# A mixture-of-experts loop over 32-token groups: from pairs to quads of groups, with one gather and one scatter for four, in the experts' natural order

## What is computed

```python
    def expert_block(args):
        rows, wts, e = args
        hgu = tok[rows] @ w_gu[e] + b_gu[e]
        gate = jnp.minimum(hgu[:, 0::2], SWIGLU_LIMIT)
        up = jnp.clip(hgu[:, 1::2], -SWIGLU_LIMIT, SWIGLU_LIMIT)
        act = (up + 1.0) * (gate * jax.nn.sigmoid(SWIGLU_ALPHA * gate))
        y = act @ w_down[e] + b_down[e]
        return y.astype(jnp.float32) * wts[:, None]
```

## Time and profile before

| | |
|---|---|
| median of 3 runs | 1428.87 us |
| the profiled execution | 1430.1 us, span 1428.3 us |
| mean granted TensorE clock | 0.917 |
| PE busy | 1201.5 us, 84% of the span |
| DVE, ACT busy | 266.6 us (19%), 230.9 us (16%) |
| chain that ended last | PE 60%, DMA 34%, issue 3% |
| DMA | 455.98 MB, mean 319 GB/s |

### The profile page before, as it was taken

How to read it: one execution, slowest core, us unless ns; L and a number is a source line. 1 busy time by engine, 2 the same in 40 slices (tenths; PEclk the granted TensorE clock), 3 DMA queues, 4 the chain that set the end, 5 groups by cost and what they waited for, 6 DMA issues and landing times.

```text
span 1428.3 us, 19043 instructions
## 1 busy us (share of the span) xinstructions
PE 1201.5 (84%) x7477; PEld 540.9 (38%) x7478; DVE 266.6 (19%) x786; ACT 230.9 (16%) x529; POOL 18.5 (1%) x26
## 2 busy tenths in 40 slices
PE   8999999999799766899999778696788797976677
PEld 4655868885433212333333122132222232312122
DVE  3335243632411100111111001010111011100001
ACT  2134423350111000111111011011011111100001
POOL 1100010000000000000000000000000000000000
PEclk9999999999799898989998989899898899988989
DMA  9933264223898999948527989989999999899993
GB/s 344 314 118 118 77 250 145 78 98 139 347 377 358 426 424 425 420 170 344 244 118 323 424 337 427 428 356 426 427 413 426 428 417 428 346 425 425 427 424 129
DMA packets 66265, 455.98 MB, mean 319 GB/s; under 512 B 7284, under 2 KB 13016, under 8 KB 33432
## 3 DMA queue, kind: packets, MB, share of 16 engines
q1 hardware_dynamic: 65528, 454.13, 77.6%
q0 software_dynamic: 256, 0.79, 0.2%
q10 hardware_dynamic: 448, 0.60, 0.1%
HBM read 454.45 MB, written 1.05 MB: 319 GB/s over the span
## 4 chain that ended last, share of the span: by engine, by line
PE 60%; DMA 34%; issue 3%; DVE 1%; ACT 1%; SPq 0%; ACTq 0%; DVEq 0%
DMA ring<-in_w_down 29%; PE bank L1005 16%; PE bank L1032 9%; PE bank L557 6%; PE bank L697 6%; DMA ring<-in_w_gu 5%; PE bank L972 4%; PE bank L980 4%; PE bank L991 2%; PE bank L606 2%; PE bank L893 2%; PE bank L859 2%; PE bank L546 1%; PE bank L583 1%; PE bank L881 1%
## 5 line engine op out<-in xcount | busy, mean ns | idle before, releaser
L1005 PE MATMUL bank<-ring,sp_ 128*32 128x512 f32 x2944 | 409.7, 688 | 134.0 <-DMA ring<-in_w_gu 80.2
L1032 PE MATMUL bank<-ring,mq 128*32 128x512 f32 x1472 | 184.5, 635 | 65.0 <-DMA ring<-in_w_down 62.6
L1005 PEld LDWEIGHTS bank<-ring,sp_ 128*32 128x32 f32 x2944 | 91.4, 119 | 372.3 <-issue 245.7
L1775 DVE TENSOR_SCALAR sp_<-bank 128x256 f32<-128x256 f32 x46 | 19.5, 425 | 858.5 <-PE bank L1005 858.5
L1032 PEld LDWEIGHTS bank<-ring,mq 128*32 128x32 f32 x1472 | 46.3, 114 | 195.5 <-issue 100.4
L972 PEld LDWEIGHTS bank<-sp_,sc 128*128 128x128 f32 x736 | 88.0, 199 | 24.3 <-issue 24.3
L972 PE MATMUL bank<-sp_,sc 128*128 128x64 f32 x736 | 91.1, 284 | 2.0 <-DVE sp_ L1758 2.0
L980 PE MATMUL bank<-mq,sp_ 128*128 128x512 f32 x184 | 86.1, 611 | 1.5 <-ACT sp_ L1363 1.5
L557 PE MATMUL bank<-ring 128*128 128x512 f32 x192 | 83.2, 592 | 0.0
L1336 ACT ACTIVATE mq<-bank 64x512 f32<-64x512 f32 x46 | 27.1, 589 | 318.6 <-PE bank L1032 318.6
L697 PE MATMUL bank<-ring 128*128 128x256 f32 x320 | 71.3, 381 | 0.0
(11 more groups left out here) (292 smaller groups left out, 818.3 us busy)
## 6 DMA issues: line engine op xcount, KB each, us to landing
ring<-in_w_gu SPq DMA_DIRECT2D x128, 2048.0 KB, 27.0
ring<-in_w_down SPq DMA_DIRECT2D x64, 2048.0 KB, 21.5
ring<-in_w_in SPq DMA_DIRECT2D x13, 2048.0 KB, 10.8
ring<-in_w_out SPq DMA_DIRECT2D x2, 2048.0 KB, 8.2
ring<-in_w_mem_kv SPq DMA_DIRECT2D x2, 1024.0 KB, 6.9
ring<-in_w_mem_kv SPq DMA_DIRECT2D x1, 2048.0 KB, 8.0
ring<-in_cmp_w_k SPq DMA_DIRECT2D x1, 2048.0 KB, 8.2
ring<-in_cmp_w_v SPq DMA_DIRECT2D x1, 2048.0 KB, 9.6
```

The source lines that it names most:

```text
L1005: mm = nc.tensor.matmul(BH[par][32 * s:32 * s + 32, :], xgT[:, k, 32 * par:32 * par + 32], w[:, c, 512 * s:512 * s + 512], start=k == 0, s ...
L1032: mm = nc.tensor.matmul(BG[64 * hh + 32 * two:64 * hh + 32 * two + 32, :], actT[par][:, o:o + 32], w[:, 2 * c + two, 512 * hh:512 * hh + 512],
L1775: V.tensor_scalar(gt[par], h[:, :, 0], LIMIT, None, ALU.min).then_inc(S("g_clip"), 1)
```

## The change

The loop body handles four groups (a quad) in place of two. `gather` picks 128 token rows at once (16 matmuls of 128 columns, both banks full) at the start of its quad, `scatter` runs once for four groups. Each group still has an If with both versions. `down` is cut into 32 matmuls of 256 columns that sum all of an expert's 8 slices in PSUM, so that ACT copies four pieces of 32x256 where it copied two of 64x512. DVE builds `Gm` with one instruction and `Gw` with two for a quad, in place of four each for a pair. A quad's four expert indices come packed in one value: two loads where there were five. 45 groups become 48 with three empty ones: `PADS` names the seats whose expert gets an empty group more, on its own weights (3, 5, 27), and `SEATS` is the order of the experts, here the natural one. In front of the loop, DVE and PE work out seats, starts and packs in more steps than the ranking needed before; SP loads three indices a round in place of one.

```diff
+QUAD = 4
+QUADS = ITEMS // QUAD
+PADS = (3, 5, 27)
+SEATS = list(range(NE))
...
-            def gather():
-
+            def gather(j, first):
+
+                pe.wait_ge(S("G_ready"), j + 1)
                 for half, b in ((0, BX), (1, BG)):
+                    if half and not first:
+                        pe.wait_ge(S("y_evac"), j * QUAD - 1)
                     for c in range(4):
                         for t in range(NT):
                             o = P * (4 * half + c)
-                            mm = nc.tensor.matmul(b[:, 64 * c:64 * c + 64], x2[:, t, o:o + P], Gm[:, t, :],
-                                                  start=t == 0, stop=t == NT - 1)
+                            mm = nc.tensor.matmul(b[:, P * c:P * c + P], x2[:, t, o:o + P],
+                                                  Gm[:, t].rearrange("p g n -> p (g n)"), start=t == 0, stop=t == NT - 1)
                     mm.then_inc(S("g_full"), 1)
...
-                            for hh in range(2):
-                                mm = nc.tensor.matmul(BG[64 * hh + 32 * two:64 * hh + 32 * two + 32, :], actT[par][:, o:o + 32],
-                                                      w[:, 2 * c + two, 512 * hh:512 * hh + 512],
-                                                      start=d + c == 0, stop=d + c == 2, skip_group_check=True)
+                            for s in range(4):
+                                mm = nc.tensor.matmul(BG[32 * s:32 * s + 32, 0:256], actT[n % 2][:, o:o + 32],
+                                                      w[:, 2 * c + two, 256 * s:256 * s + 256],
+                                                      start=d + c + two == 0, stop=d + c + two == 3, skip_group_check=True)
                     mm.then_inc(S("down_done"), 1)
...
+            def quad(j, first=False):
+
+                pack = pe.value_load(idx[0:1, bass.ds(j + AT_PACK, 1)], min_val=0, max_val=NE ** QUAD - 1)
+                at_seat = [(pack >> (5 * n)) & 31 for n in range(QUAD)]
                 if not first:
...
+                    seat_before = pe.value_load(idx[0:1, bass.ds(j + (AT_PACK - 1), 1)], min_val=0, max_val=NE ** QUAD - 1) >> 15
+                gather(j, first)
+
+                def group(n, row):
+                    if n == 0:
+                        pe.wait_ge(S("g_evac"), j * 2 + 1)
+                    up(0, at_seat[n], n, row)
+                    bias(n % 2, row)
+                    if n > 0:
+                        turn(j * QUAD + (n - 1), n - 1)
+                    elif not first:
+                        turn(j * QUAD - 1, QUAD - 1, j - 1)
+                    up(1, at_seat[n], n, row)
+                    if n == 0:
+                        pe.wait_ge(S("g_evac"), j * 2 + 2)
+                    if n > 1:
+                        pe.wait_ge(S("y_evac"), j * QUAD + (n - 1))
+                    if n > 0:
+                        down(j * QUAD + (n - 1), at_seat[n - 1], n - 1)
+                    elif not first:
+                        down(j * QUAD - 1, seat_before, QUAD - 1)
+                    up(2, at_seat[n], n, row)
+                    up(3, at_seat[n], n, row)
+
+                for n in range(QUAD):
+                    with pe.If((at_seat[n] & 1) > 0):
+                        group(n, 1)
+                    with pe.Else():
+                        group(n, 0)
+                    if n == 0 and not first:
+                        pe.wait_ge(S("y_evac"), j * QUAD)
+                        pe.wait_ge(S("st_evac"), j)
+                        scatter()
+
...
-            pair(0, first=True)
-            with pe.Fori(1, last_pair) as j:
-                pair(j)
...
+            quad(0, first=True)
+            with pe.Fori(1, last_quad + 1) as j:
+                quad(j)
...
                 act.wait_ge(S("down_done"), i * 2 + 2)
-                nc.scalar.activation(y_sb[64 * par:64 * par + 64, 0:512], BG[0:64, :], ACT.Copy)
-                nc.scalar.activation(y_sb[64 * par:64 * par + 64, 512:1024], BG[64:P, :], ACT.Copy).then_inc(S("y_evac"), 1)
+                for s in range(4):
+                    ins = nc.scalar.activation(y_sb[32 * n:32 * n + 32, 256 * s:256 * s + 256], BG[32 * s:32 * s + 32, 0:256],
+                                               ACT.Copy)
+                ins.then_inc(S("y_evac"), 1)
```

More of the change, by code:

```diff
@@ L167, in const_table @@
     add("pcol", p[:, None].astype(np.float32))
-    add("odd", (p % 2)[:, None].astype(np.float32))
+    n = np.arange(NE)
+    key = (NE - 1 - n + np.where(n == 0, 1 << 20, 0) + np.where(n == 1, 1 << 19, 0)).astype(np.float32)
+    add("key", np.tile(key, (P, 1)))
+    add("keycol", key[:, None])
+    add("seat", np.tile(np.array(SEATS, np.float32), (P, 1)))
+    later = [sum(m > x for x in PADS) for m in range(NE + 1)]
+    add("later", np.tile(np.array(later[:NE] + later[1:], np.float32), (P, 1)))
+    add("pack", np.tile(np.float32(NE) ** np.arange(QUAD, dtype=np.float32), (P, 1)))
     return np.concatenate(cols, 1), parts
@@ L1357, in _, with quad @@
-            results(last_pair * 2 - 1, 1)
-            gates(last_pair * 2, 0)
-            gates(last_pair * 2 + 1, 1)
-            results(last_pair * 2, 0, last_pair)
-            results(last_pair * 2 + 1, 1)
+                for s in range(4):
+                    ins = nc.scalar.activation(y_sb[32 * n:32 * n + 32, 256 * s:256 * s + 256], BG[32 * s:32 * s + 32, 0:256],
+                                               ACT.Copy)
+                ins.then_inc(S("y_evac"), 1)
+            def quad(j, first=False):
+                tokens(j)
+                if not first:
+                    results(j * QUAD - 1, QUAD - 1)
+                for n in range(QUAD):
+                    gates(j * QUAD + n, n)
+                    if n < QUAD - 1:
+                        results(j * QUAD + n, n, j if n == 0 and not first else None)
@@ L1363, in _ @@
+            act.wait_ge(S("idx_ready"), 1)
+            last_quad = act.value_load(idx[0:1, AT_LAST:], min_val=NE // QUAD - 1, max_val=QUADS - 1)
+            quad(0, first=True)
+            with act.Fori(1, last_quad + 1) as j:
+                quad(j)
+            results(last_quad * QUAD + (QUAD - 1), QUAD - 1)
             nc.scalar.activation(sg[0][:, 0:1], sg[0][:, 1:2], ACT.Copy).then_inc(S("last_y"), 1)
@@ new lines, in _ @@
+            step(V.tensor_scalar(Hs, n32, seat, None, ALU.is_equal))
+            arrived(dve, "first")
+            step(V.tensor_copy(total, bank("first")[0:NE, 2 * NE:2 * NE + 1]))
+            fours = C("iota")[0:NE, :].rearrange("p (k four) -> p k four", four=QUAD)[:, :, 0]
+            step(V.tensor_scalar(few, fours, total, None, ALU.is_lt))
+            step(V.tensor_reduce(quads, few, AX.X, ALU.add))
+            step(V.scalar_tensor_tensor(out=pad, in0=quads, scalar=float(QUAD), in1=total, op0=ALU.mult, op1=ALU.subtract))
@@ L1784, in pair, with quad @@
-            def pair(j, first=False, final=False):
+                V.scalar_tensor_tensor(out=u, in0=u, scalar=1.0, in1=g, op0=ALU.add, op1=ALU.mult).then_inc(S("act_ready"), 1)
+            def quad(j, first=False, final=False):
                 if not final:
```

311 lines of the change are left out of this document (137 added, 174 removed).

## The result

The changed kernel takes **1492.85 us**, the median of 4 runs (1489.33 to 1495.27), against 1429.62 us before (4 runs): a ratio of 1.0435, 95% interval 1.04 to 1.0471. It is slower by 63 us. The forecast was 1475, with a range of 1368 to 1500.

The account below looks back on a forecast made before the run. PE was taken to bound experts 6 to 9, data mostly elsewhere. With the loop's code not held, 1430 + 17 + 59 + 8 - 9 + 2 = 1507, lowered to 1475 for jumps that find code or wait unseen; range 1368 to 1500.

Parts of the forecast that it names:

- The case: PE's loop code is not held, so jumps wait for it: 1475 us, own range 1440 to 1510, chance 0.60.
- (g): PE's loop grows from 3.8 to 9.2 code packets, touching ten; if not held, jumps wait 5.5 us and a group takes 19.
- What the queue covers: While a jump waits for code, PE works on queued instructions, hiding between 1.3 and 2.7 us a time.
- Hot stretch: Experts 6 to 9, where PE bounds: idle weight queues go from 75 to 92 us with code not held, +17.
- Two-group experts and first rounds: With code not held, eight two-group experts lose 84 us against 25 before, +59, and the loop's first rounds +8.
- (a): Gather and scatter once per four groups: a gather still about 3.8 us, the two 1.87 us per group against 3.75.
- (b): Gap at the loop's head: fewer index loads remove 2.52 us idle and 1.5 us slow clock; per group 2.0 becomes 0.1.
- (c): Down as 32 matmuls 256 wide: the same 3.6 us, or 4.28 at worst, 8 us in the hot stretch.
- (e): DVE's additional small steps ahead of the loop delay the first gather by 2 us; SP's extra index loads hide.
- (f): Pads: 48 groups, empty ones behind experts 3, 5 and 27; no empty group at the end saves 13.8 us.
- the second sum: Total with code not held: 1507 us with every jump missing, 1480 with a third of the targets still there.
- The first rival: The loop's code is held, 14.0 us a group in place of 18.1: 1370 us, chance 0.31.

Follow-up runs that it names:

- experiment 3: Kernel before the change, with four never-run blocks of 75 matmuls each put into PE's loop behind an If: 1831.39 us.
- experiment 5: Changed kernel with turn and down written once outside the If, down back at 16 matmuls of 512 columns, halves summed by ACT and DVE: 1361.02 us.
- experiment 8: Kernel of experiment 5 with turn and down put back on both sides of the If, one If a group: 1455.58 us.
- experiment 9: Kernel of experiment 5 with a never-run block of 32 matmuls ahead of PE's loop, which begins half a packet later: 1433.01 us.
- experiment 1: Changed kernel with turn and down of every group moved out of the If, so that they stand once in the program: 1427.78 us.
- experiment 2: Changed kernel with turn and down moved out of the If for the first two groups of a quad alone: 1464.56 us.
- experiment 7: Kernel before the change, with two never-run blocks of 75 matmuls a pair in PE's loop: 1523.07 us.

## Why the prediction was right

**The case was the right one, and for its reason.** (g) named the loop's size, the queue for code, and the jumps; experiments 3, 5, 8 and 9 each show it, from either side. Its sizes: 141 packets against a forecast of 80 to 130. It is the loop anew behind each of the ten jumps back, 110 packets and so 11 a round; the "ten touched" of the prediction would have given 100 of them, had I multiplied. Waits: "four or five jumps of a quad wait 5.5 us each, some 24 us" was 38 in twelve quads, 17 us a quad. They were fewer than forecast, three a quad in place of four or five, and of the forecast length, 5.4 us in the mean. The jump back was the longest with 7.4 us, and I hadn't set it apart from the Ifs.

**What the queue covers** was put too high for the jump back, at 1.3 to 2.7 us a wait. The 7.07 us wait at 693 us left 6.17 us idle, so some 1 us was covered. Experiments 1 and 9, in which only the jump back waits, have 65 and 70 us of waits and are 67 and 72 us above experiment 5: what the queue covers, the slow clock behind the hole costs again. The waits at the Ifs are another matter. Experiments 8, 2 and the change have 125, 123 and 203 us of waits and are only 95, 104 and 132 us above experiment 5. Take off the jump back whole (71, 68 and 72 us), and 23, 35 and 60 us are left for 54, 55 and 132 us of waits at Ifs. So about half of these shows; this is an estimate by subtraction, good to some 7 us for each kernel. The quad came out right all the same (78 and 70 us against 76), by fewer waits that cost more each: two errors that cancelled, and so luck.

**Where it was lost.** Hot stretch: 92 us of idle forecast, 78 measured. Two-group experts and first rounds: +67 forecast, (154 - 78) - (93 - 74) = +57 measured. Both were a little high, and the sum of all jumps missing, 1507, was 14 us above the result. I had taken a third of the targets as still there and got 1480, then gone down to 1475, and the result is 18 us above that. With 11 packets a round nothing survives from one round to the next, and the waits of the jump back don't hide behind data. The argument for hiding (that PE has 15 us of slack in each one-group expert) failed on this: the jump back comes once in four groups, and where it falls at a two-group expert there is none. Experiment 9 shows it: from 800 to 1000 us its DMA share is 0.91, where experiment 5 has 1.01. The idle lies from 830 to 850 and from 930 to 950 us, behind the jumps back at 819.2 and 918.4 us, which follow experts 12 and 15 with two groups each.

**The parts.** (a) and (b): In experiment 5 the gather takes 3.84 us for 128 columns, and the gap at the loop's head is gone. Right. (c) Down at 256 columns: 3.64 for 3.6. Right. (e) The first gather came at 385.9 us, not at 381.7: +4.2 us for the +2 forecast; it now stands behind the first index load too (at 385.2 us), and I had seen this move as a gain alone. (f) An empty group in the hot stretch 13.8 us (14), in the tail 11.0 us against 13.8 forecast: the term was too high. The change's own tail gained 34.9 - 26.2 = 8.7 us, where the second sum had -14 + 5 for a jump. The size is right, the cause isn't: no branch waits there, and it is the lower clock in down and scatter (2.5 and 1.7 us more than before) that takes most of the 5 us.

**The first rival** (code held, 1370 us) comes nearest to experiment 5: 1361. It was 9 us too slow, about the ten for a first round through code that hasn't come. Experiment 5 pays nothing of the kind: its branches are all below 0.33 us, in the first round too, though there its code comes for the first time. The change itself paid it: its If waited six times before the first jump back at 538.5 us, 32 us in all. So both sums of the prediction were good to some 15 us, and what lay between them was one question, which the trace of the kernel before could not answer: it had never had more than five or six packets in its loop.

## What to carry to other kernels

Count the instructions of a loop body, both sides of every If, before you unroll it further: on PE a loop that touched seven packets of 256 instructions (an fp32 matmul is four) stayed, and one that touched eight was fetched anew, in each round or, in experiment 7, in every second. Look at the queue of kind "instruction" and at the longest compare-and-branch of the loop; 5 to 8 us there, with "issue" in front of the first matmul behind a jump, is missing code. What then helps is to write each part that both sides share once, and to see where the loop begins: 1493 became 1428 by the one, and a half-packet shift was worth 72 us.

## What I had not expected of the hardware

A block of code that never runs and stands outside the loop can cost 5% (experiment 9, 1361 to 1433 us). When the loop is one packet too long, the whole of it comes anew (nine packets a round), not the one that doesn't fit; in experiment 7 it does so in every second round, and why is open. And straight running through missing code costs nothing that the trace shows: in experiment 1 code came in every round, and only the jump back waited for more than 0.8 us.
